# Latent attentions: weights turned without their division, outputs multiplied by spread reciprocal sums, VectorE copying the second head's turned weights

## The reference

```
s = jnp.einsum('bqhgd,bkhd->bhgqk', qi, k).astype(jnp.float32) * scale
p = jax.nn.softmax(s, axis=-1).astype(v.dtype)
return jnp.einsum('bhgqk,bkhd->bqhgd', p, v)
```

## Time and profile before

| | |
|---|---|
| median of 3 runs | 2983.47 us (2981.71 to 2989.58) |
| the profiled execution | 2982.49 us |
| its span, first to last instruction | 2980.7 us |
| TensorE busy | 2848.9 us (96%) |
| mean granted TensorE clock | 0.976 |
| attention of layer 0 | 1661.8 to 1739.1 us of the span |
| attention of layer 1 | about 2669.9 to 2720.2 us of the span |

### The profile page before, as it was taken

One profiled execution on the slowest core, in us unless ns is written; L12 is line 12 of the kernel. 1 busy time (PEld: TensorE's weight loads), 2 busy tenths in 40 slices (PEclk: granted clock), 3 DMA queues, 4 the chain that ended last, 5 costly groups with the idle time before them and its releaser, 6 DMA issues.

```text
span 2980.7 us, 40307 instructions
## 1 busy us (share of the span) xinstructions
PE 2848.9 (96%) x16892; PEld 2377.2 (80%) x16892; DVE 1796.0 (60%) x2675; ACT 1158.7 (39%) x1552; POOL 192.0 (6%) x172
## 2 busy tenths in 40 slices
PE   6999999998999998999999889999999999998998
PEld 5887678786867786888888578888888888887998
DVE  4555359656634786737662668737677376546554
ACT  3333347534433664222332553212432224345443
POOL 0000000000000000000130221000120001302000
PEclk8999999999899999999999999999999999999999
DMA  7647789846377983434432013435324353321352
GB/s 297 251 174 306 277 305 366 304 147 265 156 293 259 359 330 135 178 138 174 143 107 71 29 43 113 171 122 194 134 104 179 134 185 135 105 100 57 125 193 79
DMA packets 77910, 539.77 MB, mean 181 GB/s; under 512 B 8753, under 2 KB 9009, under 8 KB 18721
## 3 DMA queue, kind: packets, MB, share of 16 engines
q1 hardware_dynamic: 76016, 529.87, 48.1%
q0 software_dynamic: 1712, 7.33, 0.9%
HBM read 536.12 MB, written 1.05 MB: 180 GB/s over the span
## 4 chain that ended last, share of the span: by engine, by line
PE 85%; DVE 6%; ACT 4%; DMA 2%; issue 2%; POOL 1%; SPq 0%; DVEq 0%; ACTq 0%
PE bank L1072 10%; PE bank L1332 9%; PE bank L1333 9%; PE bank L1334 9%; PE bank L1367 5%; PE bank L1369 5%; PE bank L1368 5%; PE bank L1267 4%; PE bank L1269 4%; PE bank L1268 4%; PE bank L1487 2%; PE bank L1292 2%; PE bank L1294 2%; PE bank L1259 2%; PE bank L1293 2%; DMA raw<-in_w_mods 2%
## 5 line engine op out<-in xcount | busy, mean ns | idle before, releaser
L2169 DVE TENSOR_TENSOR w_lo<-raw,w_hi 128x2048 fp32r<-128x2048 f32 (+1 forms) x356 | 773.0, 2173 | 311.1 <-ACT w_hi L1685 310.4
L1685 ACT ACTIVATE w_hi<-raw 128x2048 fp32r<-128x2048 f32 (+1 forms) x356 | 645.8, 1816 | 526.5 <-PE bank L1369 240.6
L1332 PE MATMUL bank<-h_hi,w_hi 128*128 128x512 f32 (+1 forms) x1472 | 528.0, 359 | 20.4 <-DVE h_lo L2335 12.7
L1334 PE MATMUL bank<-h_hi,w_lo 128*128 128x512 f32 (+1 forms) x1472 | 524.9, 357 | 0.0
L1333 PE MATMUL bank<-h_lo,w_hi 128*128 128x512 f32 (+1 forms) x1472 | 524.8, 357 | 0.0
L1332 PEld LDWEIGHTS bank<-h_hi,w_hi 128*128 128x128 f32 x1472 | 281.2, 191 | 64.7 <-DVE h_lo L2335 11.9
L1333 PEld LDWEIGHTS bank<-h_lo,w_hi 128*128 128x128 f32 x1472 | 281.2, 191 | 38.6
L1334 PEld LDWEIGHTS bank<-h_hi,w_lo 128*128 128x128 f32 x1472 | 281.0, 191 | 38.7
L2221 DVE CUSTOM_DVE_ANT_0 bank<-raw,raw 128x1024 f32<-128x1024 f32 x240 | 286.3, 1255 | 0.0
L1367 PE MATMUL bank<-act_hi,w_hi 128*128 128x512 f32 (+1 forms) x770 | 270.0, 351 | 0.9 <-DVE w_lo L2169 0.9
L1927 ACT ACTIVATE quads<-bank 128x512 f32<-128x512 f32 (+1 forms) x88 | 47.9, 544 | 570.9 <-PE bank L1334 570.9
(11 more groups left out here) (471 smaller groups left out, 4561.2 us busy)
## 6 DMA issues: line engine op xcount, KB each, us to landing
raw<-in_w_experts SPq DMA_DIRECT2D x192, 1024.0 KB, 6.6
raw<-in_w_ffn_in SPq DMA_DIRECT2D x88, 1024.0 KB, 4.8
raw<-in_w_mods SPq DMA_DIRECT2D x60, 1024.0 KB, 7.2
raw<-in_w_wide SPq DMA_DIRECT2D x60, 1024.0 KB, 4.8
raw<-in_w_ffn_out SPq DMA_DIRECT2D x64, 704.0 KB, 4.1
raw<-in_w_c_in SPq DMA_DIRECT2D x20, 1024.0 KB, 4.8
raw<-in_w_a_in SPq DMA_DIRECT2D x12, 1024.0 KB, 6.4
raw<-in_w_b_in SPq DMA_DIRECT2D x12, 1024.0 KB, 5.4
```

Source lines behind the costliest of these rows:

```text
L1332: pe.matmul(o, hi[:, f, :], h_hi[:, k, cols], start=(k == 0), stop=False)
L1334: mm = pe.matmul(o, lo[:, f, :], h_hi[:, k, cols], start=False, stop=(k == KT - 1))
L1685: act.activation(w_hi[pair_of(k)][:, 0:size], raw_of(k)[:, 0:size], ACT.Copy).then_inc(sem("hi_ready"), 1)
L2169: dve.tensor_tensor(w_lo[pair_of(k)][:, 0:size], raw_of(k)[:, 0:size], w_hi[pair_of(k)][:, 0:size].bitcast(F32), ALU.subtract).then_inc(*r ...
```

## The change

The unit's softmax is no longer divided before it is turned. In its place:

- TensorE turns `g_p` as soon as its exponentials are there. It waits for ScalarE's and VectorE's copies of the unit before. Before the product of unit u-3 it also spreads the reciprocal sums: two matmuls of the broadcast column `g_inv` with the identity write, into the other columns of the output's bank, the reciprocal of each query's sum on all rows of a head.
- ScalarE copies only the first head's turned weights, then copies the raw output of unit u-4 from PSUM to `g_raw`, and rounds `g_out` of unit u-5 to `h_hi`.
- VectorE computes the reciprocal of unit u-1 into `g_inv`, copies the second head's turned weights of unit u-2 (`g_pt`), and multiplies `g_raw` of unit u-4 with the spread reciprocals, which gives `g_out`. `h_lo` is now that of unit u-6, from `g_out`.

```
@@ TensorE
-                        pe.wait_ge(*W("mix_v", ("probs", v)))
+                        pe.wait_ge(*W("mix_a", ("exp", v)))
                         if v:
                             pe.wait_ge(*W("mix_a", ("turned", v - 1)))
+                            pe.wait_ge(*W("mix_v", ("turned", v - 1)))
...
                         pe.wait_ge(*W("mix_a", ("turned", v)))
+                        pe.wait_ge(*W("mix_v", ("turned", v)))
                         if v >= 2:
-                            pe.wait_ge(*W("h_ready", v - 2))
+                            pe.wait_ge(*W("mix_v", ("out", v - 2)))
+                        pe.wait_ge(*W("mix_v", ("inverse", v)))
+                        for x in range(2):
+                            pe.matmul(psum[6 + v % 2][64 * x:64 * x + 64, P:T1], g_inv[v % 4][:, x:x + 1].broadcast_to([P, 64]), ident,
+                                      start=True, stop=True, skip_group_check=True)
@@ ScalarE
-                        for x in range(2):
-                            ins = act.activation(g_pt[v % 2][:, x, 0:nt, :].rearrange("p t n -> p (t n)"), psum[2 + x][:, 0:P * nt], ACT.Copy)
-                        ins.then_inc(*T("mix_a", ("turned", v)))
-                    if u >= 3:
-                        v = u - 3
+                        act.activation(g_pt[v % 2][:, 0, 0:nt, :].rearrange("p t n -> p (t n)"), psum[2][:, 0:P * nt], ACT.Copy)\
+                            .then_inc(*T("mix_a", ("turned", v)))
+                    if 4 <= u < len(us) + 4:
+                        act.wait_ge(*W("product", ("out", u - 4)))
+                        act.activation(g_raw[u % 2], psum[6 + u % 2][:, 0:P], ACT.Copy).then_inc(*T("mix_a", ("out", u - 4)))
+                    if u >= 5:
+                        v = u - 5
                         s, pair, qb = us[v]
-                        act.wait_ge(*W("product", ("out", v)))
-                        act.activation(h_hi[:, pair, T1 * s + P * qb:T1 * s + P * qb + P], psum[6 + v % 2][:, 0:P], ACT.Copy)\
+                        act.wait_ge(*W("mix_v", ("out", v)))
+                        act.activation(h_hi[:, pair, T1 * s + P * qb:T1 * s + P * qb + P], g_out[v % 2], ACT.Copy)\
@@ VectorE
-                    if u >= 4:
-                        v = u - 4
+                    if u >= 6:
+                        v = u - 6
...
-                        dve.tensor_tensor(h_lo[:, pair, cut], psum[6 + v % 2][:, 0:P], h_hi[:, pair, cut].bitcast(F32), ALU.subtract)\
+                        dve.tensor_tensor(h_lo[:, pair, cut], g_out[v % 2], h_hi[:, pair, cut].bitcast(F32), ALU.subtract)\
...
                         dve.wait_ge(*W("mix_a", ("exp", v)))
-                        step(dve.reciprocal(stt[:, 4:6], stt[:, 2:4]))
-                        for x in range(2):
-                            p = g_p[v % 3][:, x, 0:k1 - k0]
-                            ins = dve.tensor_scalar(p, p, stt[:, 4 + x:5 + x], None, ALU.mult)
-                        ins.then_inc(*T("mix_v", ("probs", v)))
+                        if v >= 4:
+                            dve.wait_ge(*W("product", ("out", v - 4)))
+                        dve.reciprocal(g_inv[v % 4], stt[:, 2:4]).then_inc(*T("mix_v", ("inverse", v)))
+                    if 2 <= u < len(us) + 2:
...
+                        dve.wait_ge(*W("product", ("turn", v)))
...
+                        dve.tensor_copy(g_pt[v % 2][:, 1, 0:nt, :].rearrange("p t n -> p (t n)"), psum[3][:, 0:P * nt]).then_inc(*T("mix_v", ("turned", v)))
+                    if 4 <= u < len(us) + 4:
+                        v = u - 4
+                        dve.wait_ge(*W("mix_a", ("out", v)))
+                        if v >= 2:
+                            dve.wait_ge(*W("h_ready", v - 2))
+                        dve.tensor_tensor(g_out[v % 2], g_raw[v % 2], psum[6 + v % 2][:, P:T1], ALU.mult).then_inc(*T("mix_v", ("out", v)))
```

More of the change, by code:

```diff
@@ L330, in build @@
         g_tap = g("g_tap", [P, T2])
+        g_raw, g_out = ([g(f"g_{n}{i}", [P, P]) for i in range(2)] for n in ("raw", "out"))
         assert g.pos[0] <= y_at + KT * T2 * 4
@@ L338, in build @@
         g_st = [small[:, 8 * i:8 * i + 8] for i in range(2)]
+        g_inv = [inv8[:, 2 * i:2 * i + 2] for i in range(4)]
         def ada_row(name):
@@ L1617, in attention @@
                                 mm = pe.matmul(psum[6 + v % 2][64 * x:64 * x + 64, 0:P], g_v[:, k0 // P + t, c0:c0 + 64],
-                                               g_pt[v % 2][:, x, t, :], start=(t == 0), stop=(t == nt - 1))
+                                               g_pt[v % 2][:, x, t, :], start=(t == 0), stop=(t == nt - 1), skip_group_check=True)
                         mm.then_inc(*T("product", ("out", v)))
@@ L2085, in attention @@
                 us = units(l)
-                for u in range(len(us) + 3):
+                for u in range(len(us) + 5):
                     if u < len(us):
@@ L2914, in attention @@
                 us = units(l)
-                for u in range(len(us) + 4):
+                for u in range(len(us) + 6):
                     if u < len(us):
@@ L2937, in attention @@
                         v = u - 1
-                        k0, k1 = keys_of(us[v][0])
                         stt = g_st[v % 2]
                         dve.wait_ge(*W("mix_a", ("exp", v)))
-                        step(dve.reciprocal(stt[:, 4:6], stt[:, 2:4]))
-                        for x in range(2):
-                            p = g_p[v % 3][:, x, 0:k1 - k0]
-                            ins = dve.tensor_scalar(p, p, stt[:, 4 + x:5 + x], None, ALU.mult)
-                        ins.then_inc(*T("mix_v", ("probs", v)))
+                        if v >= 4:
+                            dve.wait_ge(*W("product", ("out", v - 4)))
+                        dve.reciprocal(g_inv[v % 4], stt[:, 2:4]).then_inc(*T("mix_v", ("inverse", v)))
+                    if 2 <= u < len(us) + 2:
+                        v = u - 2
+                        nt = (keys_of(us[v][0])[1] - keys_of(us[v][0])[0]) // P
+                        dve.wait_ge(*W("product", ("turn", v)))
+                        if v >= 2:
+                            dve.wait_ge(*W("product", ("out", v - 2)))
+                        dve.tensor_copy(g_pt[v % 2][:, 1, 0:nt, :].rearrange("p t n -> p (t n)"), psum[3][:, 0:P * nt]).then_inc(*T("mix_v", ("turned", v)))
+                    if 4 <= u < len(us) + 4:
+                        v = u - 4
+                        dve.wait_ge(*W("mix_a", ("out", v)))
+                        if v >= 2:
+                            dve.wait_ge(*W("h_ready", v - 2))
+                        dve.tensor_tensor(g_out[v % 2], g_raw[v % 2], psum[6 + v % 2][:, P:T1], ALU.mult).then_inc(*T("mix_v", ("out", v)))
             def turn_out():
```

## The result

The changed kernel takes 2993.35 us (median of 7 runs, 2984.04 to 2995.74), the kernel before 2985.35 us (7 runs, 2981.71 to 2989.58). The ratio is 1.0024, 95% interval 1.0012 to 1.0035: by this ratio it is slower by 7.2 us, with 3.6 to 10.4 possible.

What follows compares the result with a forecast made beforehand. The prediction held the attentions bound by the order in which three engines hand units on, not load. Layer 0 +5.3, layer 1 +3.6 and 0.3 for waits gave +9.2 on 2983.5: 2992.7 us, range 2986.5 to 2998.5.

Steps and rivals of the forecast that it cites:

- The closed loop: Attention units: ScalarE and VectorE take turns within one pass; 4.47 us a biased unit, 2.48 short; chance as priced 0.45.
- The sum over units: Steady units: layer 0 units 6 to 12 +4.1, 12 to 23 +1.5; layer 1 units 6 to 11 +3.4 us.
- The filling: Pipeline start, units 0 to 6: -0.9 us in layer 0 (bounds 0 and -1.2), -0.2 in layer 1.
- an excess of 1.15 in these two: Layer 0's first two division pairs take 1.43 and 1.48 us, later ones 0.88; removing them was to save 0.9.
- the loop of 3.67: ScalarE and VectorE taking turns in a unit without bias, 3.67 us; claimed not to bind in units 0 to 6.
- The end: Last output of each attention passes an extra copy and multiplication: +0.6 us in layer 0 (bounds +0.2 and +0.9), +0.4 in layer 1.
- a reserve for unpriced waits: Over both attentions: 0.3 us added for more waits that TensorE and VectorE process, bounds 0 and 1.
- the bound of 0.3%: Whole program: slower by over 0.3%, above 2992.4 us, had chance 0.52; within 0.43; faster by over 0.3% 0.05.
- the loads decide: Rival, attention units: VectorE finds `g_raw` ready, long units run at TensorE's 3.4 us; -6.6 us, 2976.9; chance 0.06.
- Clock falls over whole attentions: Rival: TensorE at its lower clock level in the attentions, passes over 5 us; 15 us more, 3007; chance 0.07.
- the cheaper loop: Rival, attention units: shorter ScalarE handover or short units held by something else; if short units lose half, +7.5 us; chance 0.30.
- the loop at full durations: Rival, new handovers: copies and multiplications cost full durations without overlap; 0.2 us more a unit, +4.5, 2997; chance 0.12.

Runs made afterwards that it cites:

- `g_raw` first: Changed kernel with ScalarE's copy to `g_raw` (unit u-4) and rounding to `h_hi` (u-5) moved ahead of the exponentials of unit u: 2974.86 us, ratio 0.9971.
- ScalarE copies both: Changed kernel with ScalarE copying both heads' turned weights and VectorE none: 3008.33 us, ratio 1.0091 to the kernel before.
- spread twice: Changed kernel with the two spreading matmuls issued twice per unit: 2990.61 us, ratio 1.0032 to the kernel before.
- the new order: Changed kernel, TensorE's product (u-4) ahead of turns (u-2), ScalarE's exponentials last, VectorE's pass reordered: 2961.72 us, ratio 0.9932 to the kernel before.

## Why the prediction was right, and where not

**The closed loop**: right in kind and size. Forecast 4.47 and 2.48 us, measured 4.45 and 2.48. That the handover closes it is shown by `g_raw` first (no work taken away, loop gone), that ScalarE's copy lies in it by ScalarE copies both (+0.49), that the spreading does not by spread twice (+0). Every term read from the earlier trace rows came within 0.01.

**The sum over units**: units 6 to 12 took 25.91 (forecast 26.0) and 12 to 23 28.70 (28.5), so +4.0 and +1.65 against +4.1 and +1.5; layer 1 from unit 6 to 11 22.56 (22.7), +3.3 against +3.4.

**The filling**: the step that failed, "I take **-0.9** of an excess of 1.15 in these two", of layer 0. Measured -0.1. The slow divisions were taken for the reason of the filling's length because they were the row that looked long; with fast ones the kernel before filled in 19.86 in place of 19.81. The sentence "the loop of 3.67 does not bind" failed with it: from unit 4 on it binds. The lower clock of the earlier trace rows lengthens this filling in both kernels and does not explain the miss. In layer 1 -0.2 was forecast and +0.3 measured, but there the clocks differ (1.00 before, 0.72 changed); at 0.72 the same code of before took 20.12, and against that it is -0.3. By the rule of the Trainium skill ("SBUF — State Buffer", "Who interferes with whom") the term would have been -1.2, further off still.

**The end**: +0.6 and +0.4 forecast, +1.0 (beyond the bound of 0.9) and +0.5 measured. These lines of the changed kernel answer to the earlier trace rows:

```profile
1747.25 0.28 ACT L2119 ACTIVATE g_raw<-bank 128x128 f32<-128x128 f32 x1 [0.75 <-PE bank L1626]
...
1747.56 0.29 DVE L2966 TENSOR_TENSOR g_out<-g_raw,bank 128x128 f32<-128x128 f32 x1 [0.68 <-ACT g_raw L2119]
...
1747.88 0.31 ACT L2124 ACTIVATE h_hi<-g_out 128x128 fp32r<-128x128 f32 x1 [0.16 <-DVE g_out L2966]
...
1748.22 0.29 DVE L2945 TENSOR_TENSOR h_lo<-g_out,h_hi 128x128 fp32r<-128x128 f32 x1 [0.18 <-ACT h_hi L2124]
```

From `g_raw` to `h_hi` are 0.63, as forecast (0.64). The other 0.4 lie in the last short units, and spread twice adds 0.4 there again: TensorE's spreading has no cover at the end, which the forecast gave it everywhere.

**The sum and the median**: forecast 9.2, of which 0.3 was a reserve for unpriced waits; 10.6 in the stretches of the two profiled executions. The missed terms, 1.3 (filling, 0.5 of it in layer 1 and the clock's) and 0.5 (end), less 0.3, make up the difference but for 0.1. With both layers 1 at a clock of 0.72 the attentions cost 10.0. By the ratio the whole program lost 7.2 (3.6 to 10.4). That 2992.7 came so close to 2993.35 is luck in part: the median before rose from 2983.47 to 2985.35 with more runs, and what lies outside the attentions took back what they cost beyond the forecast. The ratio's interval lies across the bound of 0.3%.

**The rivals**: the loads decide (0.06) was wrong of this kernel, but its 3.4 us is what the new order reaches. Clock falls over whole attentions did not come (0.98 and 0.97, the kernel before 0.98 and 1.00). Steps of 4.45 and 2.48 leave no room for the cheaper loop, nor for the loop at full durations, which would be 0.2 longer.

## What to carry to other kernels

Where two engines work through fixed lists, write down for each wait of which pass its producer is: a value that is made and read in the same pass, between a wait in one direction and a wait in the other, closes a loop whose length is the sum of both engines' steps, and saved work elsewhere gives nothing. Place what is ready ahead of what must wait: here order alone was worth 17.7 us of the attentions with the old arithmetic and 23.9 with the new, against 10.6 for the change. Before blaming a long row, look at who waits for it, and compare two stretches only at the same granted clock.

## What the runs showed of the hardware

Identical code ahead of the first changed instruction took 1658.06 to 1670.02 us in the profiled executions, 12 us, more than the effect studied; the stretches of the attentions repeat more closely (layer 0 77.34 and, with a changed GpSimd only, 77.42), but not without the clock: layer 1, with no change at all, 50.34 at 1.00 and 50.97 where the first units had 0.72. Pauses of 2 us on TensorE in the filling were followed by a granted clock of 0.66 to 0.72 (3 to 9 us behind the first scores) in most fillings, and of 1.00 in layer 1 of the kernel before and of three others; eight idle matmuls of 2.05 us in all held 1.00 in both layers. VectorE's copy of 128x512 from PSUM took 0.67, as the nearest row had it.
